# A two-block transformer kernel on one core: the rotation of the third-kind mixers' queries and keys moved half a chunk later on VectorE

## What is computed

```python
h = rms_norm(x, norm1_g[l])
z = h @ w_in[l]                      # 1024 x 8704
zq, zf, zi, zg, zatt, za, zb = jnp.split(z, split_idx, axis=-1)
o_hg = hgrn2_chunked(q_hg, log_f, k_hg, v_hg)          # a gated linear recurrence
qkv = zatt.reshape(B, S, 3, N_GROUPS, ATT_HEADS, ATT_DIM)
for g, (window, dilation) in enumerate(ATT_GROUPS):    # 3 groups of 4 heads
    qg = partial_rope(qkv[:, :, 0, g], cos, sin)       # rotates 32 of the 128 dimensions
    kg = partial_rope(qkv[:, :, 1, g], cos, sin)
    o_g, lse_g = dilated_window_attention(qg, kg, qkv[:, :, 2, g], window, dilation)
y = (sigmoid(za) * (o_hg @ w_branch_a[l]) + sigmoid(zb) * (o_att @ w_branch_b[l]))
x = x + y @ w_out[l]
```

## Time and profile before

| | |
|---|---|
| median of the runs | 1879.49 us |
| the profiled execution | 1879.31 us, of which its span is 1877.5 us |
| PE busy | 1863.6 us, 99% of the span |
| DVE busy | 1265.3 us, 67% |
| ACT busy | 944.4 us, 50% |
| POOL busy | 62.9 us, 3% |
| PE 128x512 matmul `stream<-whi,x_split` (L2365) | 395 ns, 944 of them |
| DVE rest of one block (L1313) | 1222 ns, 582 of them |
| ACT split of one block (L786) | 1056 ns, 582 of them |

### The profile page before, as it was taken

The page is one execution under the profiler, slowest core; times in us unless marked ns, Lnnn a source line. Parts: engine busy times, 40 slices in busy tenths (PEclk is TensorE's granted clock), DMA queues, the critical chain, the costliest instruction groups (busy, mean ns, idle before and its releaser), DMA issues.

```text
span 1877.5 us, 25275 instructions
## 1 busy us (share of the span) xinstructions
PE 1863.6 (99%) x9637; PEld 1586.2 (84%) x9637; DVE 1265.3 (67%) x1559; ACT 944.4 (50%) x1225; POOL 62.9 (3%) x94
## 2 busy tenths in 40 slices
PE   9999999999999999999999999999999999999998
PEld 7888988888888898888889888888889888888886
DVE  4466786466546668745576997677656797776754
ACT  5454574554345446445446545545444645445543
POOL 1010100000000000000000000000000000000000
PEclk9999999999999999999999999999999999999999
DMA  9667545656665665666555554455665554465562
GB/s 327 193 195 218 196 140 193 192 181 186 207 195 183 180 187 145 207 198 184 181 173 185 164 181 143 134 193 186 201 192 174 181 191 159 133 190 170 189 191 79
DMA packets 173656, 342.58 MB, mean 182 GB/s; under 512 B 10992, under 2 KB 11168, under 8 KB 173424
## 3 DMA queue, kind: packets, MB, share of 16 engines
q1 hardware_dynamic: 169376, 327.26, 56.1%
q0 software_dynamic: 4176, 13.90, 2.3%
HBM read 338.49 MB, written 1.05 MB: 181 GB/s over the span
## 4 chain that ended last, share of the span: by engine, by line
PE 88%; DVE 10%; issue 1%; ACT 1%; POOL 0%; POOLq 0%; DVEq 0%; ACTq 0%
PE stream L2365 18%; PE stream L2367 18%; PE stream L2366 18%; PE stream L2560 6%; PE stream L2561 3%; PE aux L2418 3%; DVE wlo L1313 3%; PE stream L2540 3%; PE stream L2541 3%; PE stream L2542 3%; PE stream L2403 2%; PE stream L2394 1%; PE stream L2395 1%; PE stream L2477 1%; PE stream L2479 1%; PE stream L2478 1%
## 5 line engine op out<-in xcount | busy, mean ns | idle before, releaser
L1313 DVE TENSOR_TENSOR wlo<-raw,whi 128x1024 fp32r<-128x1024 f32 x582 | 703.8, 1222 | 472.2 <-ACT whi L786 469.3
L786 ACT ACTIVATE whi<-raw 128x1024 fp32r<-128x1024 f32 x582 | 607.1, 1056 | 543.6 <-PE stream L2367 429.6
L2365 PE MATMUL stream<-whi,x_split 128*128 128x512 f32 x944 | 373.3, 395 | 1.5 <-DVE ak L1324 0.6
L2367 PE MATMUL stream<-whi,x_split 128*128 128x512 f32 x944 | 368.1, 390 | 0.0
L2366 PE MATMUL stream<-wlo,x_split 128*128 128x512 f32 x944 | 367.5, 389 | 0.0
L2365 PE MATMUL stream<-whi,hhi 128*128 128x512 f32 x672 | 263.3, 392 | 0.0
L2367 PE MATMUL stream<-whi,hlo 128*128 128x512 f32 x672 | 261.6, 389 | 0.0
L2366 PE MATMUL stream<-wlo,hhi 128*128 128x512 f32 x672 | 261.5, 389 | 0.0
L2560 PE MATMUL stream<-x_split,whi 128*128 128x512 f32 x672 | 241.4, 398 | 2.8 <-DVE ak L1324 2.1
L2367 PEld LDWEIGHTS stream<-whi,x_split 128*128 128x128 f32 x944 | 177.2, 188 | 37.9
L2365 PEld LDWEIGHTS stream<-whi,x_split 128*128 128x128 f32 x944 | 177.3, 188 | 37.3 <-DVE x_split L1349 1.5
(11 more groups left out here) (345 smaller groups left out, 2105.9 us busy)
## 6 DMA issues: line engine op xcount, KB each, us to landing
raw<-ffn_w_gu SPq DMA_DIRECT2D x175, 512.0 KB, 4.4
raw<-w_in SPq DMA_DIRECT2D x136, 512.0 KB, 4.6
raw<-ffn_w_down SPq DMA_DIRECT2D x88, 512.0 KB, 3.8
raw<-w_up SPq DMA_DIRECT2D x64, 512.0 KB, 4.4
raw<-w_down SPq DMA_DIRECT2D x64, 512.0 KB, 4.3
raw<-c_w_in SPq DMA_DIRECT2D x24, 512.0 KB, 3.9
raw<-ab_w_in SPq DMA_DIRECT2D x20, 512.0 KB, 4.9
raw<-w_out SPq DMA_DIRECT2D x16, 512.0 KB, 3.7
```

The lines of the kernel that those rows point to most:

```text
L786: act.activation(split_slots(lin, at, j)[0], raw[:, b % RAW], ACT.Copy).then_inc(hi_ready, 1)
L1313: dve.tensor_tensor(lo, raw[:, b % RAW], hi.bitcast(F32), ALU.subtract).then_inc(lo_ready, 1)
L2365: pe.matmul(bank[tt][:], hi, wh, start=kt == 0, stop=False)
L2367: mm = pe.matmul(bank[tt][:], lo, wh, start=False, stop=kt == last)
```

## The change

The three instructions of the rotation leave `use(c)` and become a function `rotate(c)`. It is called from the `within` hook of the following chunk ahead of block 2, so that it comes after the rests of blocks 0 and 1 and after `add_halves`, and ahead of the rests of blocks 2 and 3. It is called with `c - 1`, so each rotation works on the same data, with the same semaphores, as before.

```diff
-                    if 5 <= c <= 10:
-                        group = (c - 5) % 3
-                        part = (aq if c < 8 else ak)[0:32, 4 * group:4 * group + 4]
-                        ...
                     if c == 13:
                         head_copies()
+
+                def rotate(c):
+
+                    group = (c - 5) % 3
+                    part = (aq if c < 8 else ak)[0:32, 4 * group:4 * group + 4]
+                    other = rope_swap[c % 2]
+                    seen.swaps += 1
+
+                    dve.wait_ge(swap_in[c % 2], 32 * ((seen.swaps + 1) // 2))
+                    shape = [32, 4, S]
+                    step(dve.tensor_tensor(other[:], other[:], over(cst("sin_b", 32), shape), ALU.mult))
+                    step(dve.tensor_tensor(part, part, over(cst("cos_b", 32), shape), ALU.mult))
+                    dve.tensor_tensor(part, part, other[:], ALU.add).then_inc(roped, 1)
+                    seen.roped += 1
...
-                layer(into, use, beside(into, -48), lambda c: tiles_from(aq if c < 7 else ak, 4 * ((c - 4) % 3)))
+                later = beside(into, -48)
+
+                def within(c, j):
+                    if 6 <= c <= 11 and j == 2:
+                        rotate(c - 1)
+                    later(c, j)
+
+                layer(into, use, within, lambda c: tiles_from(aq if c < 7 else ak, 4 * ((c - 4) % 3)))
```

## The result

The changed kernel takes **1909.66 us** (median of 5 runs, 1909.4 to 1911.33) where the kernel before takes 1879.48 on the same chip; the ratio is 1.0163, 95% interval 1.0149 to 1.0177. The forecast was 1909.4 us, in a range of 1903 to 1914. The profiled execution took 1909.66 us, of which its span is 1907.8.

A forecast was written before the change was run, and what follows sets the result against it. DVE was taken to bound the rotations' stretch. A layer loses 12.9 us of DVE delay plus 2.3 for the clock less 0.2 slack, 15.0; two layers 30.0, giving 1909.4 us, range 1903 to 1914.

The forecast's parts named there:

- The bound: In the stretch of the rotations DVE, busy 79.19 of 79.90 us, is fuller than PE, so its idle time counts.
- 6 x 2.07: DVE idles 2.07 us behind `decay_to` for ACT's split, six times a layer: 12.4 us.
- The third add: After chunk 5's side work, the third add waits for ACT's third copy: 0.5 us idle, once a layer.
- 12.9: DVE's delay at the end of the stretch, 12.4 + 0.5 us a layer, reaching the first turn of chunk 12.
- The wait ahead of the logits: At the head of chunk 12 PE stands idle for 6.4 us, waiting for the sixth rotation.
- The clock: PE's clock falls in the wait ahead of chunk 12's logits: 2.3 us, less 0.2 of slack, a layer.
- The waits at chunks 8 to 10: PE waits 2.5 to 2.9 us at each start of chunks 8, 9 and 10; the clock may fall or not.
- The clock stays up: Rival: no clock fall at chunk 12, or a shorter PE idle time; 2 x 12.9 = 25.8 us, 1905.2 us; chance 0.25.
- The clock costs more: Rival: both blocks at half speed, or late rests add PE waits; up to 4 us more a layer, 1913 to 1917; chance 0.10.
- Faster: Rival: PE's waits at the starts of chunks 7 to 10 go, 3.4 us, so 1876.1 us; chance 0.02.
- nothing: Rival: the moved rotation only shifts the waits, as DVE's work is the same; about 1879 us; chance 0.02.

The follow-up runs named there:

- experiment 4: Changed kernel with each rotation worked on 32 of 256 tokens only, the rest of it left out: 1873.17 us, ratio 0.9968.
- experiment 1: Changed kernel with ACT's exponential of the recurrence moved behind the splits of blocks 0 and 1 and the three copies: 1888.6 us, ratio 1.0048.
- experiment 3: Changed kernel with two of each rotation's three instructions kept behind `decay_to` and one behind the adds ("two kept"): 1879.48 us, ratio 1.0001.
- 7: ACT's exponential of levels 2 to 8 on a quarter of its elements: in the changed kernel 1904.28 us, in the kernel before 1879.23.
- experiment 5: Changed kernel with matmuls that nobody reads filling PE's wait ahead of chunk 12's logits; with 26 of them 1906.21 us, ratio 1.0143.
- 2: Changed kernel with the first of each rotation's three instructions put back behind `decay_to`, two left behind the adds: 1896.34 us, ratio 1.0092.
- both of 6: Kernel before with only some rotations moved: those of chunks 5 to 7, 1895.33 us; only the last, of chunk 10, 1884.98 us.
- first run of 5: Changed kernel with 50 matmuls that nobody reads ahead of PE's wait for the sixth rotation in chunk 12: 1915.49 us.
- both of 8: POOL instead of DVE: sine product of each rotation in the kernel before, 1888.96 us; whole rotation in the changed kernel, 1920.47 us.

## Why the prediction was right, point by point

- **The bound.** That DVE is the bound in this stretch, at 67% over the whole span, is shown by experiment 4: the same idle times cost nothing as soon as DVE has less to do.
- **6 x 2.07.** The idle time came out at 2.07 or 2.08 us six times a layer, as read from its one example in the earlier trace rows. Experiments 1, 3 and 7 show its cause: without the exponential in between it is gone, under two instructions of cover it is gone, and with a shorter exponential it is shorter by just that.
- **The third add** waits 0.40 us, once in a layer; 0.5 was in the sum.
- **12.9 was a little low.** The reciprocal of chunk 12 is 13.43 us later in the first layer. The idle times and the add make 12.8. The missing 0.6 shows when `decay_to` is followed from chunk to chunk: its delay grows by 2.15 to 2.17 us in each. Two instructions of DVE that follow each other overlap by some 0.08 us (the rotation of the earlier trace rows starts at 1044.66, while `decay_to` before it ends at 1044.06 + 0.68 = 1044.74); where DVE stands idle between them, this is lost as well. I had counted the idle time and not the overlap.
- **The wait ahead of the logits:** 6.20 us and 6.4 in the second layer, 6.4 predicted. This is in part luck, as both of its ends were put too early. Chunk 11 starts at 1108.92 and not at 1107.7, since it follows the level work of chunk 10 and does not wait for a rest, and it takes 11.0 us with nothing for late rests, so PE is through 1.0 us later; the sixth rotation is over 0.6 us later, by the overlaps.
- **The clock** fell there, as predicted. Its price was 2.3 less 0.2 = 2.1 us in the sum. Measured are 14.92 - 13.43 = 1.5 us in the first layer and 15.42 - 13.46 = 2.0 in the second, and 1.4 and 1.9 by experiment 5. The two errors, 0.55 too little for DVE's delay and 0.35 too much on average for the clock, nearly cancel: 15.0 predicted, 14.92 and 15.42 measured. Part of the hit is luck.
- **The waits at chunks 8 to 10** were to be 2.5 to 2.9 us. They are 2.70, 0.96 and 2.23. I had left open whether the clock falls there; it fell around the first, so chunk 8 took longer and PE was less early at chunk 9. As argued, this is hidden: PE only uses up its own wait. The second layer of experiment 5 with 26 shows the same place without the fall: behind 2.71 us the clock stays at 1.00, and PE then waits 2.23 us at chunk 9 instead of 0.94.
- **The rivals.** "The clock stays up" is what experiment 5 made by hand: 1906.2, where 1905.2 was its price. "The clock costs more" did not come: net it took 1.5 and 2.0 us where the forecast had 2.1, and no late rest held PE in chunk 11. "Faster" and "nothing" needed an idle time under 0.3 us at the rest, or slack of DVE; experiment 3 is a kernel in which the first holds, and it gives before's time, not less.

Of the expectations, those of experiments 1, 2 and both of 6 were too low by the same omission in part: I summed DVE's delay and took it that the clock would not fall where PE's wait was shorter than 6 us. In 1 the adds came too early as well. The first run of 5 missed by the length of its fillers, 7 by a second wait that the first had hidden, and in both of 8 the rival came true.

No kernel here beats the kernel before with all its work done; two kept is equal to it.

## What to carry to other kernels

Work that stands between a producer and the answer of another engine is cover for the latency of that answer. To price a move, look for the place in the trace where the same pair already stands without cover, read the idle time there, and multiply; only so much of the moved work must stay as the chain is long (here 2 of 3 instructions). The same work can cover a second wait that shows only when the first is gone (the adds in experiment 1). Whether an idle time counts is decided by whether its engine is full in that stretch, not by its share of the span. And a wait that makes PE idle can have a second price behind it, the lower clock, which is paid only where PE, or an engine that waits for PE, has no slack afterwards.

## What the runs showed of the hardware

- Whether the granted clock falls was not decided by the length of PE's wait alone. In chunks 6 to 12 of both layers, over all the traces, it stayed at 1.00 behind every wait up to 1.70 us (the whole rotation on POOL), and fell to 0.50 with every wait from 3.16 us on (there too), up to 9.15. In between the same wait does both. 2.70 us brought it down in chunk 8 of after; 2.71 in the second layer of experiment 5 with 26 did not. 2.23 us did in chunk 10 of after; 2.24 at the same place of the second layer did not. 2.06 us did with the last rotation only; 2.05 in its second layer did not. 1.79 us did with the sine on POOL; 1.90 did not. I had expected a fall only for the longest and left the others open; what decides in between stays open.
- In some of these the clock fell only after PE had started again: in chunk 10 of after PE starts at 1095.46, and the 128x512 matmuls are slow from 1096.51 on.
- With the clock at 0.50, 128x512 matmuls took 0.63 us at a spacing of 0.43, where 0.39 and 0.23 are usual, for 2.9 us after PE's start (experiment 1, second layer) up to 6.1 (the first three moved, chunk 10). So one fall has no fixed price.
- A tensor_tensor of 32x1024 on POOL lasts 2.4 to 3.4 us, and one of DVE's beside it took 3.43 instead of 1.21, ending 1.09 us after POOL's.
- Consecutive DVE instructions overlap by about 0.08 us, so an idle time costs a little more than its own length: 2.15 to 2.17 us for 2.07.
